# A hybrid decoder step on one NeuronCore: the front reordered by kinds of products, an own PSUM bank for weighted rows, two free half pages per head pair

## What is computed

```python
def rms_norm(x, g):
    return x * rsqrt(mean(x * x) + EPS) * g

qkv_raw, z, b, a, q_down, kv_down, gates = split(rms_norm(x, norm_mix) @ w_in)
q = rms_norm(q_down, q_a_norm) @ w_uq              # 8 heads of 128 + 64
qn, qr = rms_norm(q[:128], q_norm_nope), rope(rms_norm(q[128:], q_norm_rope))
c  = rms_norm(kv_down[:512], kv_a_norm)
kr = rope(rms_norm(kv_down[512:], k_norm_rope))
kn, v = rms_norm(c @ w_uk, k_norm_nope), c @ w_uv  # prompt, and every cached row
# each sample token attends to 16 cached pages of 128 rows, c and kr from the cache:
# scores = (qn . kn + qr . kr) * scale, softmax over pages, sum of v
```

## Time and profile before

| what | value |
|---|---|
| median of 3 runs | 1555.3 us (1554.84 to 1557.21) |
| profiled execution | 1555.73 us, its span 1553.9 us |
| PE busy | 1501.8 us, 97% of the span |
| ACT, DVE, POOL busy | 867.4, 831.0, 203.8 us |
| chain that ended last | PE 87%, DVE 5%, ACT 5%, issue 2% |
| DMA | 174.44 MB, 112 GB/s on the mean |

### The profile page before, as it was taken

How to read it: one execution, slowest core, us unless ns; L and a number is a source line. 1 busy time by engine, 2 the same in 40 slices (tenths; PEclk the granted TensorE clock), 3 DMA queues, 4 the chain that set the end, 5 groups by cost and what they waited for, 6 DMA issues and landing times.

```text
span 1553.9 us, 27023 instructions
## 1 busy us (share of the span) xinstructions
PE 1501.8 (97%) x9292; PEld 1230.0 (79%) x9292; DVE 831.0 (53%) x1639; ACT 867.4 (56%) x2795; POOL 203.8 (13%) x104
## 2 busy tenths in 40 slices
PE   6997999999999999999999999999999999999998
PEld 4875767776877867778678777787777999999998
DVE  5765434555445554455554455635423466777643
ACT  2323566757656676575766566666767344344332
POOL 0000111111221111121111111113122100000000
PEclk9999999999999999999999999999999999999999
DMA  7514123542234632346333453222634446555551
GB/s 242 165 51 108 35 74 82 132 112 60 66 65 119 142 88 63 65 97 139 86 65 74 104 131 70 59 62 68 181 71 120 142 163 238 186 162 171 186 188 57
DMA packets 265826, 174.44 MB, mean 112 GB/s; under 512 B 167576, under 2 KB 214200, under 8 KB 265560
## 3 DMA queue, kind: packets, MB, share of 16 engines
q1 hardware_dynamic: 261094, 170.72, 41.4%
q10 hardware_dynamic: 4602, 2.06, 0.6%
HBM read 132.62 MB, written 6.74 MB: 90 GB/s over the span
## 4 chain that ended last, share of the span: by engine, by line
PE 87%; DVE 5%; ACT 5%; issue 2%; ACTq 1%; DMA 0%; DVEq 0%
PE ps L1847 14%; PE ps L1849 14%; PE ps L1848 14%; PE ps L2252 5%; PE ps L2253 5%; PE ps L2254 5%; PE ps L1870 2%; PE ps L1941 2%; PE ps L2200 2%; PE ps L2201 2%; PE ps L2202 2%; PE ps L1942 1%; PE ps L1943 1%; PE ps L1888 1%; PE ps L2007 1%
## 5 line engine op out<-in xcount | busy, mean ns | idle before, releaser
L749 ACT ACTIVATE ksq<-ps 128x128 f32<-128x128 f32 x1024 | 268.9, 277 | 318.0 <-PE ps L1849 317.0
L1847 PE MATMUL ps<-ukh,cTh 128*128 128x512 f32 x1024 | 419.6, 410 | 5.8 <-DVE cTl L1118 5.8
L1849 PE MATMUL ps<-ukh,cTl 128*128 128x512 f32 x1024 | 401.9, 392 | 0.0
L1848 PE MATMUL ps<-ukl,cTh 128*128 128x512 f32 x1024 | 401.1, 392 | 0.0
L651 POOL TENSOR_TENSOR rk<-kss,mhalf 128x32 f32<-128x32 f32 x32 | 178.4, 5576 | 521.2 <-DVE kss L1546 521.2
L1847 PEld LDWEIGHTS ps<-ukh,cTh 128*128 128x128 f32 x1024 | 193.2, 189 | 60.7 <-issue 16.1
L1849 PEld LDWEIGHTS ps<-ukh,cTl 128*128 128x128 f32 x1024 | 192.8, 188 | 43.0
L1848 PEld LDWEIGHTS ps<-ukl,cTh 128*128 128x128 f32 x1024 | 193.5, 189 | 34.5
L749 ACT ACTIVATION_READ_ACCUMULATOR ksq<-ps 128x1 f32 x1024 | 211.5, 207 | 0.0
L737 ACT ACTIVATE cTr<-turned 128x1024 uint16<-128x1024 uint16 x128 | 176.2, 1377 | 17.5 <-DMA turned<-planes 10.7
L1118 DVE TENSOR_TENSOR cTl<-cTr,cTh 128x512 fp32r<-128x512 f32 x128 | 88.3, 690 | 133.1 <-ACT cTh L740 131.4
(11 more groups left out here) (481 smaller groups left out, 2741.8 us busy)
## 6 DMA issues: line engine op xcount, KB each, us to landing
clat<-cache_mla SPq DMA_DIRECT2D x128, 256.0 KB, 2.5
wraw<-w_in SPq DMA_DIRECT2D x16, 1024.0 KB, 5.0
wraw<-w_up SPq DMA_DIRECT2D x16, 1024.0 KB, 5.4
wraw<-w_down SPq DMA_DIRECT2D x16, 1024.0 KB, 5.0
braw<-w_in SPq DMA_DIRECT2D x24, 512.0 KB, 4.0
crope<-cache_mla SPq DMA_DIRECT2D x128, 32.0 KB, 2.3
sst<-state_gdn SPq DMA_DIRECT2D x32, 128.0 KB, 3.1
gdn_sample<-sst SPq DMA_DIRECT2D x32, 128.0 KB, 2.3
```

The lines of the kernel that those rows point to most:

```text
L749: i = nc.scalar.activation(ksq[:, P * h:P * h + P], ps[:, k % 3, P * h:P * h + P], ACT.Square, accum_out=kss[:, n // 4 % 2, n % 4, 4 * hal ...
L1847: mm(out, cTh[:, n % 2, c], ukh[:, c, cols], start=c == 0, stop=False)
L1848: mm(out, cTh[:, n % 2, c], ukl[:, c, cols], start=False, stop=False)
L1849: i = mm(out, cTl[:, n % 2, c], ukh[:, c, cols], start=False, stop=c == 3)
```

## The change

- **x.** The eight turned pieces go to eight banks and are drained by DVE (even) and ACT (odd). Five products of a constant tile stand ahead of the first transposition. xn and its split are made in two halves, the high part on ACT. The DMA issues of the norm vectors move from SP to ACT's queue, those of the small weights (wmisc), tables and page table from ACT's queue to SP's, behind the first units.
- **Products by kind.** For units 0 to 3 `half_unit` does 16 products high by high, then 16 high by x's low part, then 16 with the weights' low part, each kind with its own wait. Unit 2 has its own tiles `w2h`, `w2l`.
- **Scale.** kv, qd and the rope rows are no longer multiplied by rx. Since rms_norm(s*y) with epsilon is y*rsqrt(mean(y*y) + EPS/(s*s)), their roots add `xeps` = EPS*(mean(x*x)+EPS) instead. rx itself is made after qd.
- **Sums.** For x, kv and qd POOL adds the squares pairwise (8 or 4 chunks to 1) and PE does one product in place of 8, 4 and 4. `head_sums` writes 32-column windows into the four quarters of a bank; one root serves nope and rope rows.
- **Drains.** ACT drains kv and qd, each bank by a square and a scaled copy, and the banks of kn, qn and qr; DVE keeps those of v.
- **Start of the loop.** Pages 0 and 1 are turned by PE, not by the transposing DMA. Page loads are issued earlier and in fours.
- **Loop.** Weighted rows and turned latents get bank 3 (bank 4 for the last two groups), `weigh` no longer waits for the score parts, `rope_columns` no longer for `lacc` and its sum, and `latent_columns` stands one page later. STEPS has an empty half page between steps 13 and 14 and between 16 and 17 of each pair: 49 half pages a pair, 8 more in all, out of those left over at the end of the loop.

```diff
+BY_ACT = [True] * 28 + [False] * 4
+XBANK = [0, 1, 2, 3, 5, 6, 7, 4]
...
+STEPS = list(range(14)) + [None, 14, 15, 16, None] + list(range(17, 47))
...
+def head_row(j):
+    return 32 * (j % 4) + j // 4 if j < 16 else 32 * ((j - 16) // 2) + 4 + j % 2
...
+    b, k = divmod(k, B_SLOTS)
+    return (b, STEPS[k]) if 0 <= b < HP and STEPS[k] is not None else (None, None)
...
+        def sum_bank(gg):
+            return ps[:, 3 if gg < NG - 2 else 4, :]
...
+                if n == 4:
+                    sp.wait_ge(S("pool_clear"), 1)
+                    for c0, src in ((0, win[:, :, OFF_ROPE:OFF_ROPE + 64]), (64, win[:, :, OFF_ROPE:OFF_ROPE + 64]),
+                                    (128, win[:, :, OFF_BETA:OFF_BETA + 8]), (160, win[:, :, OFF_BETA + 8:OFF_BETA + 16])):
+                        sp.dma_start(wmisc[:, :, c0:c0 + src.shape[2]], src).then_inc(S("wmisc_landed"), 16)
+                if n == 6:
+                    sp.dma_start(consts[:, C_COS.start:], C_in[:, C_COS.start:]).then_inc(S("tables_landed"), 16)
+                    sp.dma_start(ab[32:40, 0:1], I["a_log"].rearrange("l h -> h l")).then_inc(S("ab_landed"), 16)
+                    sp.dma_start(ab[32:40, 1:2], I["dt_bias"].rearrange("l h -> h l")).then_inc(S("ab_landed"), 16)
+                    sp.dma_start(ptab[:], I["page_table"].rearrange("b g -> (b g)").rearrange("(o n) -> o n", o=1)).then_inc(S("ptab_landed"), 16)
...
+            def chunk_sum(k, c0, n):
+                g.wait_ge(S("sq_ready"), k)
+                while n > 1:
+                    n //= 2
+                    i = nc.gpsimd.tensor_tensor(sq[:, c0:c0 + n, :], sq[:, c0:c0 + n, :], sq[:, c0 + n:c0 + 2 * n, :], ALU.add)
+                    if n > 1:
+                        pool_links[0] += 1
+                        i.then_inc(S("pool_link"), 1)
+                        g.wait_ge(S("pool_link"), pool_links[0])
+                i.then_inc(S("sq_summed"), 1)
+            chunk_sum(1, 0, KC)
+            chunk_sum(2, 4, 4)
+            chunk_sum(4, 0, 4)
...
+            def weigh_banks(n, q0, x, c0, col):
+                for j in range(4):
+                    act.wait_ge(S("chunk_done"), 4 * n + j + 1)
+                    b_ = ps[:, (q0 + j) % 4, 0:T]
+                    i = nc.scalar.activation(sq[:, c0 + j, :], b_, ACT.Square)
+                    if j == 3:
+                        i.then_inc(S("sq_ready"), 1)
+                    nc.scalar.activation(x[:, j, :], b_, ACT.Copy, scale=par[:, col + j:col + j + 1]).then_inc(S("acc_act"), 1)
...
+            x_chunk(1)
+            x_chunk(3)
+            hi(0)
+            x_high(0)
+            x_chunk(5)
+            x_chunk(7)
+            hi(1)
+            act.wait_ge(S("x_even"), KC // 2)
+            act.wait_ge(S("x_odd"), KC // 2)
             square(sq[:, 0:8, :], xT[:], "sq_ready")
-            hi(0)
-            sqrt(P, side("x_sum"))
-            hi(1)
+            x_high(1)
             hi(2)
-            act.wait_ge(S("acc_read"), KC + 4)
+            hi(3)
+            act.wait_ge(S("pool_link"), 1)
+            act.wait_ge(S("side_read"), 1)
+            weigh_banks(1, 0, kv, 4, PR_KVA)
+            hi(4)
...
+            x_chunk(0)
+            x_chunk(2)
             v.wait_ge(S("side_done"), side("params"))
             V.tensor_copy(par[:, 0:PR_ALL], ps[:, 4, 0:PR_ALL]).then_inc(S("side_read"), 1)
-            v.wait_ge(S("side_read"), 1)
-            v.wait_ge(S("acc_read"), KC)
-            link(V.tensor_tensor(xn[:], xT[:], par[:, PR_MIX:PR_MIX + KC].unsqueeze(2).to_broadcast([P, KC, T]), ALU.mult))
-            split(xn[:], Ah[:], Al[:], "a_ready")
+            x_normed(0)
+            x_chunk(4)
+            x_chunk(6)
+            x_low(0)
             lo(0)
-            rsqrt("x_sum", P, rx[:], 1.0 / D, 1)
+            x_normed(1)
+            x_low(1)
             lo(1)
             lo(2)
-            for j in range(4):
-                acc(1, j, KC + j, kv[:, j, :], rx[:])
             lo(3)
-            rsqrt("kv_sum", P, rsq[:, 1], 1.0 / LAT, 2)
-            for c in range(4):
-                i = V.scalar_tensor_tensor(kv[:, c, :], kv[:, c, :], par[:, PR_KVA + c:PR_KVA + c + 1], rsq[:, 1], ALU.mult, ALU.mult)
-            link(i)
+            link(V.tensor_scalar(rx[:], side_bank("x_sum"), 1.0 / D, EPS, ALU.mult, ALU.add))
+            link(V.tensor_scalar(xeps[:], rx[:], EPS, None, ALU.mult))
+            v.sem_inc(S("side_read"), 1)
+            rsqrt("kv_sum", rsq[:, 1], 1.0 / LAT, 1, eps=xeps[:])
+            v.wait_ge(S("acc_act"), 4)
+            V.tensor_tensor(kv[:], kv[:], rsq[:, 1].unsqueeze(1).to_broadcast([P, 4, T]), ALU.mult).then_inc(S("scaled"), 1)
...
+            def half_unit(n, q0, half, beside=None):
+                cs = slice(4 * half, 4 * half + 4)
+                def products(w, x, j, last=False):
+                    for kc in range(4):
+                        i = mm(ps[:, (q0 + j) % 4, 0:T], w(n)[:, kc, 128 * j:128 * j + 128], x[:, cs][:, kc, :], start=w is hi_of and x is Ah and half == 0 and kc == 0, stop=last and kc == 3)
+                    return i
+                pe.wait_ge(S("w_hi"), n + 1)
+                pe.wait_ge(S("left_hi"), half + 1)
+                for j in range(4):
+                    if half == 0:
+                        bank(q0 + j)
+                    products(hi_of, Ah, j)
+                if beside:
+                    beside()
+                pe.wait_ge(S("left_lo"), half + 1)
+                for j in range(4):
+                    products(hi_of, Al, j)
+                pe.wait_ge(S("w_lo"), n + 1)
+                for j in range(4):
+                    products(lo_of, Ah, j, half == 1).then_inc(S("chunk_done"), 1)
...
+            pe.wait_ge(S("warm_ready"), 1)
+            for _ in range(5):
+                mm(ps[:, 7, :], warm[:, 0:P], warm[:, P:P + 512], start=True, stop=True)
...
+            def sum_of(name, k, c):
+                pe.wait_ge(S("sq_summed"), k)
+                mm(begin(name)[:, 0:T], ones, sq[:, c, :], start=True, stop=True).then_inc(S("side_done"), 1)
...
+                    r = slice(32 * (h % 4), 32 * (h % 4) + 32)
+                    i = mm(b[r, 0:T], window(r0 + h // 4, 32), sq[:, h, :], start=start and h < 4, stop=stop and h >= 4)
...
+            pe.wait_ge(S("x_even"), 2)
+            pe.wait_ge(S("x_odd"), 2)
+            half_unit(0, 0, 0)
+            half_unit(1, 0, 1)
+            half_unit(2, 4, 0)
+            sum_of("x_sum", 1, 0)
...
-                wait(pe, "acc_done", gg - 1)
-                wait(pe, "accT_ready", (gg - 1) // 4)
                 wait(pe, "s_parts", gg)
                 for m in range(2):
                     u = (4 * gg + 2 * m) % RING
-                    k = nc.tensor.transpose(ps[:, B_SUM, P * m:P * m + P], crope[:, u:u + 2, :].rearrange("p u n -> p (u n)"), ident)
+                    k = nc.tensor.transpose(ps[:, B_SCORE, P * m:P * m + P], crope[:, u:u + 2, :].rearrange("p u n -> p (u n)"), ident)
...
-                pe.wait_ge(S("s_parts"), min(gg + 2, NG))
+                if gg >= NG - 2:
+                    pe.wait_ge(S("s_parts"), NG)
                 wait(pe, "acc_done", gg)
                 wait(pe, "accT_ready", gg // 4)
                 for t in range(4):
-                    k = mm(ps[32 * t:32 * t + 32, B_SUM, :], pst[:, gg % 2, t, :], clat[:, (4 * gg + t) % RING, :], start=True, stop=True)
+                    k = mm(sum_bank(gg)[32 * t:32 * t + 32], pst[:, gg % 2, t, :], clat[:, (4 * gg + t) % RING, :], start=True, stop=True)
...
+            transposes(0)
...
-                if t == 1 and g >= 2 and g % 4 == 1:
+                if t == 2 and g >= 2 and g % 4 == 1:
                     latent_columns(g // 4 - 1)
...
```

More of the change, by code:

```diff
@@ L706, in _ @@
+            act.wait_ge(S("side_read"), side("rope_raw"))
+            square(sq[:, 8, :], krT[:], "sq_ready")
+            act.wait_ge(S("side_done"), side("x_sum"))
+            weigh_banks(3, 4, qd, 0, PR_QA)
             hi(6)
-            act.wait_ge(S("acc_read"), KC + 8)
-            square(sq[:, 4:8, :], qd[:], "sq_ready")
-            sqrt(P, side("kr_sum"))
+            drain(4, 0, 8, kn[:, 0, :])
+            sqrt(P, side("qd_sum"))
+            for j in range(1, 4):
+                drain(4, j, 8 + j, kn[:, j, :])
@@ L710, in _ @@
             hi(7)
-            sqrt(P, side("qd_sum"))
-            act.wait_ge(S("acc_read"), KC + 16)
+            drain(5, 0, 12, kn[:, 4, :])
+            act.wait_ge(S("scaled"), 2)
+            nc.scalar.activation(qdh[:], qd[:], ACT.Copy).then_inc(S("left_hi"), 1)
+            for j in range(1, 4):
+                drain(5, j, 12 + j, kn[:, 4 + j, :])
+            act.wait_ge(S("x_made"), 3)
+            nc.scalar.activation(rsq[:, 1], rsq[:, 0], ACT.Sqrt).then_inc(S("sqrt_done"), 1)
+            act.wait_ge(S("acc_act"), 16)
@@ L713, in _ @@
             act.wait_ge(S("side_done"), side("qd_sum"))
             square(sq[:, 0:8, :], kn[:], "sq_ready")
```

(52 more changed lines are left out.)

396 lines of the change are left out of this document (198 added, 198 removed).

## The result

| what | before | after |
|---|---|---|
| median | 1555.66 us (4 runs, 1554.84 to 1557.21) | 1494.42 us (4 runs, 1494.17 to 1494.75) |
| span of the profiled execution | 1553.9 us | 1492.4 us |
| start of the first weight product | 27.50 | 13.93 |
| start of the first key product | 135.79 | 100.83 |
| start of the last key product of the high parts (L1847, now L1991) | 1210.02 | 1149.32 |

The ratio is 0.9605, 95% interval 0.9589 to 0.9622: faster by 61 us. The forecast was 1505 us, 50.5 us less, with a range from 1496 to 1519. The landmarks say where: the front (to the first keys) gave 35.0 us against 34.5 forecast, the loop 25.7 against 16, and the part behind it 0.8 against nothing.

The account below looks back on a forecast made before the run. PE was taken as the bound, busy for 1501.8 of 1553.9 us. Gains of 13.9 (to first product), 11.2 (body), 9.4 (tail) and 16 (loop) made 50.5 us off 1555.7, forecast 1505 us, range 1496 to 1519.

Parts of the forecast that it names:

- To the first product: Front, up to the first weight product: its start moves from 27.5 to 13.6 us, 13.9 us gained.
- The body: Front, from first weight product to last value product: 91.8 becomes 80.6 us, 11.2 us less.
- the walk's 80.6: Front body's length in us from walking the engines' lists by the forecast durations, taken in place of the terms' sum 79.7.
- slow start: Front, first units: PE may start at its slow clock level after resting; 1.3 us charged, between nothing and 1.5 per place.
- three times the clearing: POOL's adds in the front: 2.7 ns an element, three times its clearing's 0.9; 2.1 us for qd's 792 elements.
- The tail: Front, from the last value product to the first keys: 16.5 becomes 7.1 us, 9.4 us less, first keys at 101.3.
- The loop: Loop over the pages: all five groups of listed PE waits, 17.0 us, are addressed; 16 us less.
- I give 1 us back: Loop: 1 us off the 17.0, since 49 for 47 half pages change which step meets which page of a group.
- 52 us is the most that waiting can give back, unless PE's own work shrinks: Whole kernel: PE busy for 1501.8 of 1553.9 us, so removing waits alone gains at most 52 us.
- The stage behind the loop: After the loop: no wait worth a row there, and the change moves nothing.
- Rivals 1 to 4: Front bound by DVE/ACT, 1519, 0.14; loop waits return, 1515, 0.1; slow POOL adds, 2075, 0.02; front changes fail, 1515, 0.06.
- Rival 5: Better: POOL fast, no slow start, 17 us in the loop: 1501, to 1496; within the forecast's spread, no separate chance.

Follow-up runs that it names:

- pe_sums: The changed kernel without POOL's adds: PE sums the chunks over x, kv and qd itself, the sum over x one place earlier; 1499.57 us.
- loop_only: The kernel before with the loop's changes alone (own bank, later latents, both free half pages), the front left as it was; 1533.04 us, ratio 0.9852.
- rows32: The changed kernel, but products that spread the roots of the nope rows take 32 rows, not all 128; 1496.37 us.

## Why the prediction was wrong, point by point

- **To the first product, 27.5 to 13.6.** Right: 13.93. One assumption in it was too good for the profiled execution: the five products should cover the wait for x, but the turning starts behind them at 8.49, and x had landed by 7.4 to 7.6. ACT's high parts then ran as forecast.
- **The body.** Right in sum: the last value product ends at 94.5 (forecast 94.2). The terms as written add up to 80.7, not 79.7, so the walk's 80.6 only repeats them; measured are 80.5. Head sums 1.10 us (1.1). No wait for kv's sum. Wait for qd's sum 1.70 (2.5). At the slow start, 3.5 us stand for 2.1, 1.4 more (1.3). POOL's 792 additions for qd took 2.12 us (2.1), but the rate behind that term did not hold:

```profile
L680 POOL TENSOR_TENSOR sq<-sq x2: 740/1024/1307, 48.8 to 50.2; 128x528 f32<-128x528 f32 x1, 128x264 f32<-128x264 f32 x1
```

  264 elements more cost 0.57 us, 2.15 ns an element, and each addition has some 0.17 us besides, by that; "three times the clearing", 2.7 ns with nothing fixed, met the sum by luck of the size. The rate of the Trainium skill (GPSIMD Engine Reference, 3.1 Elementwise), 4497 ns for 2048 elements, is 2.2 ns an element and agrees with the 2.15; the 1.7 us worked out from it, an estimate, is 0.4 below the trace, most of it what the two additions have besides. Beside DVE's work the sums for x and kv took 7.77 and 3.64 us for 5.0 and 2.1; both lay under PE's products, so that miss cost nothing. The advice of that page of the Trainium skill, to leave element-wise work to DVE, was not put to the test, since `pe_sums` moved the sums to PE (5 us slower).
- **The tail, 7.1 us.** Right: 94.5 to 100.83, 6.4. First keys at 100.83 against 101.3.
- **The loop, 16 us. This is the step that failed**, as "17.0 us" less "I give 1 us back". It measured 25.7. Nothing was to be given back (idle in the loop is 0.35 us), and the sum counted only listed idle time. Missing were 1.6 us of slow clock behind the `lsq` wait, some 2.2 us of overlap lost at fourteen waits (an estimate), 1.7 us of slow clock at the first keys, and 2.0 us of shape changes; these and the 17.4 us of idle make 24.9, and 0.8 us stay open. That the loop's own edits give 22 us, and that the shape of an operand gives 2, is shown by `loop_only` and `rows32`; the other three are read from rows. The slow clock at the first keys was in my rows: the products behind the earlier trace rows's 135.79 last 0.79 us, and I had priced the same thing in the front at up to 1.5 us per place and not here.
- **"52 us is the most that waiting can give back, unless PE's own work shrinks."** The condition was the case, and I didn't look at it for the loop. Idle fell by 41.9 us and busy by 19.6, where I had said some 30 and some 20; the 20 was right by luck. By stretch it is 10.4 in the front, 8.6 in the loop and 0.6 behind, and the constant products turn 7.1 us of waiting for x into busy time, which hides as much of the real fall.
- **The stage behind the loop** gave 0.8 us. The 0.8 us are missing in the profile of `loop_only`, and they come in no one place: against `loop_only`, the same products are 0.1 us ahead after 50 us of this stage and 0.85 us ahead after 320. Its cause stays open.
- **The range.** Its low end came from "POOL fast, no slow start, 17 us in the loop", so the listed waits were taken as the ceiling of the loop's term. With the lost overlap and the two slow stretches the term would have been 22.5, and the range would have reached the measured time.
- **Rivals.** Rivals 1 to 4 did not come true. The front was not bound by DVE or ACT, the loop's waits did not come back, the quarters overlap, and POOL's adds cost 2.7 ns an element when alone, all told. Rival 5 had the right side but not the reason: there was a slow start, POOL was as forecast, and the loop gave 25.7, not 17.

## What to carry to other kernels

A wait costs more than its idle time: add the overlap that products lose (their duration less their spacing, 0.16 us here) and look at the granted clock and the spacing of the products behind each longer wait. So when many waits of one engine are removed, compare its busy time too, and let the list of waits be the low end of the range, not the high one. And before a slow stretch is charged, ask which wait comes next: half pace at the first keys cost nothing as long as the third page's DMA turn came late.
